# The last projection of a hybrid mLSTM / differential-attention block with its operands exchanged, and the high parts of the weight tiles on ScalarE

## The reference, cut to what matters

```python
xn   = rmsnorm(x, pre_g)
proj = xn @ w_in                      # 1024 x 10256, split into the parts used below
h_a  = sigmoid(m_o) * rmsnorm(mlstm_forward + mlstm_backward) * silu(m_z)      # 4 heads
h_b  = rmsnorm(diff_attention(aq, ak, av)) * (1 - lam_init) * silu(a_z)        # 8 heads
g_a, g_b = split(sigmoid(g_merge + b_merge))
y    = g_a * (h_a @ w_branch_m) + g_b * (h_b @ w_branch_a)
out  = y @ w_out                      # 1024 x 1024: the last projection
return x + rmsnorm(out, post_g)       # norm over the 1024 channels of each token
```

## Time and profile before

| | us |
|---|---|
| median of three runs | 1740.48 |
| profiled execution, whole | 1740.36 |
| its span in the trace | 1738.6 |
| TensorE matmul busy | 1655.1 (95%) |
| VectorE busy | 1037.4 (60%) |
| ScalarE busy | 755.8 (43%) |
| GpSimd busy | 771.0 (44%) |

### The profile page before, as it was taken

The page is one execution under the profiler, slowest core; times in us unless marked ns, Lnnn a source line. Parts: engine busy times, 40 slices in busy tenths (PEclk is TensorE's granted clock), DMA queues, the critical chain, the costliest instruction groups (busy, mean ns, idle before and its releaser), DMA issues.

```text
span 1738.6 us, 24563 instructions
## 1 busy us (share of the span) xinstructions
PE 1655.1 (95%) x8235; PEld 1355.8 (78%) x8235; DVE 1037.4 (60%) x1692; ACT 755.8 (43%) x1462; POOL 771.0 (44%) x926
## 2 busy tenths in 40 slices
PE   4999999999999998999999999999999999999995
PEld 3788887887878877878787878787877788888784
DVE  6703676776676767787878787878776101235213
ACT  5213444444444434555555555555554113344322
POOL 3543244244253355444444454545432444567630
PEclk9999999999999999999999999999999999999998
DMA  5041112012022022121212121212121737523322
GB/s 169 13 134 30 31 49 73 24 51 70 24 60 61 25 86 61 37 61 40 57 41 55 42 54 45 52 45 51 48 61 49 254 128 259 169 74 95 121 72 97
DMA packets 137300, 129.08 MB, mean 74 GB/s; under 512 B 5089, under 2 KB 120354, under 8 KB 136226
## 3 DMA queue, kind: packets, MB, share of 16 engines
q1 hardware_dynamic: 130594, 111.66, 22.1%
q10 hardware_dynamic: 6656, 16.78, 2.5%
HBM read 90.67 MB, written 29.36 MB: 69 GB/s over the span
## 4 chain that ended last, share of the span: by engine, by line
PE 60%; DVE 19%; ACT 10%; issue 10%; DMA 1%; DVEq 1%; ACTq 0%; SPq 0%
PE ps L621 45%; PE ps L629 7%; DVE negmax L1351 2%; PE ps L803 2%; PE ps L811 2%; ACT probs L1794 2%; ACT aT_split L1799 2%; DVE aT_split L1356 1%; DMA v_f<-in_x 1%; DVE h_sum L1304 1%; DVE raw_b L1038 1%; DVE mix L1343 1%; DVE q_stack L1286 1%; DVE sigmoid_work L1038 1%; DVE h_sum L1234 1%
## 5 line engine op out<-in xcount | busy, mean ns | idle before, releaser
L621 PE MATMUL ps<-xn_split,w_split 128*128 128x512 f32 x4224 | 1032.9, 401 | 2.4 <-ACT v_f L1501 1.9
L621 PEld LDWEIGHTS ps<-xn_split,w_split 128*128 128x128 f32 x4224 | 789.5, 189 | 187.1 <-POOL w_split L560 2.3
L554 POOL TENSOR_TENSOR w_split<-w_raw,ones 128x256 fp32r<-128x256 f32 x416 | 318.8, 796 | 855.9 <-PE ps L621 812.8
L560 POOL TENSOR_TENSOR w_split<-w_raw,w_split 128x256 fp32r<-128x256 f32 x416 | 329.3, 822 | 8.2
L1794 ACT ACTIVATE probs<-ps,negmax 128x1024 f32<-128x1024 f32 x128 | 143.0, 1117 | 139.0 <-DVE negmax L1351 139.0
L621 PE MATMUL ps<-h_split,w_split 128*128 128x512 f32 x768 | 181.2, 396 | 0.1
L621 PEld LDWEIGHTS ps<-h_split,w_split 128*128 128x128 f32 x768 | 143.4, 188 | 35.1 <-issue 0.5
L1351 DVE TENSOR_REDUCE negmax<-ps 128x1 f32<-128x1024 f32 x128 | 150.2, 1214 | 4.5 <-PE ps L803 4.5
L1356 DVE TENSOR_TENSOR aT_split<-ps,aT_split 128x512 fp32r<-128x512 f32 x128 | 88.5, 691 | 90.5 <-ACT aT_split L1799 89.6
L803 PE MATMUL ps<-k_stack,q_stack 128*128 128x512 f32 x512 | 135.7, 407 | 7.0 <-DMA k_stack<-k_stack 7.0
L803 PEld LDWEIGHTS ps<-k_stack,q_stack 128*128 128x128 f32 x512 | 92.4, 191 | 25.7 <-DMA k_stack<-k_stack 5.4
(11 more groups left out here) (236 smaller groups left out, 1843.8 us busy)
## 6 DMA issues: line engine op xcount, KB each, us to landing
w_raw<-in_w_in SPq DMA_DIRECT2D x80, 512.0 KB, 3.9
k_stack<-k_stack SPq DMA_DIRECT2D x16, 512.0 KB, 4.2
spill_a<-o_split SPq DMA_DIRECT2D x32, 256.0 KB, 2.8
h_split<-spill_m SPq DMA_DIRECT2D x8, 1024.0 KB, 7.1
qk_f<-spill_g SPq DMA_DIRECT2D x16, 512.0 KB, 3.4
xn_split<-spill_a SPq DMA_DIRECT2D x8, 1024.0 KB, 6.9
spill_g<-qk_f ACTq DMA_DIRECT2D x12, 512.0 KB, 2.6
spill_m<-hT_split ACTq DMA_DIRECT2D x8, 512.0 KB, 2.9
```

The costliest lines, as they stand in the source:

```text
L554: hi = pool.tensor_tensor(wsp[b][:, 0, ks_], raw[b][:, ks_], ones[:, 0:1].unsqueeze(2).to_broadcast([P, SPLIT_K, P]), ALU.mult)
L560: lo = pool.tensor_tensor(wsp[b][:, 1, ks_], raw[b][:, ks_], wsp[b][:, 0, ks_].bitcast(F32), ALU.subtract)
L621: mm = pe.matmul(ps[:, half, :], wsp[b][:, wl, k, :], moving[:, xl, k, cols], start=(k == 0 and n == 0), stop=(k == KT - 1 and n == 2))
```

## The change

It has two parts.

**The last projection.** y is now the stationary operand, 128 tokens at a time, and w_out moves in quarters of 256 channels. Each of 32 units (quarter n, token tile t) has 24 matmuls of 256 columns and leaves tokens on partitions, so the copy to SBUF and the transposes back are gone. A quarter is made of two 128-channel tiles; GpSimd makes both their parts, into new buffers `wo[n % 2]` that lie where `ya` was. For quarter 0 it waits for four of eight y tiles, for quarter 1 for all eight, and for quarters 2 and 3 until TensorE is done with the quarter before the last. Eight PSUM banks are used in turn. Per unit VectorE multiplies by the gain and ScalarE squares and sums; in the last quarter each token tile gets its sum, its statistics, its scaling and its store two tiles behind the matmuls. The first six units begin with seven of eight y tiles.

**The high parts.** For tiles 2 to 95 the high part is one ScalarE copy of 128x1024 (`split_high`), issued right behind the read of the second half of tile g-2; GpSimd makes only the low part, and waits for that copy. SP's load of a tile waits for the low part of tile g-2, as before.

The core of the diff; AHEAD is 6, and the last loops shown are VectorE's and ScalarE's:

```diff
+            wo = [sb(f"wo_split{i}", [P, 2, KT, QUARTER], F32R, at=f_scope) for i in range(2)]
...
                 g, b = tile_no(base, per_head, h, j)
-                pool.wait_ge(raw_loaded[b], 16 * ((per_head // 2) * h + ((base + j) // 2 + 1)))
-                if not (isinstance(g, int) and g < 2):
+                if isinstance(g, int) and g < 2:
+                    pool.wait_ge(raw_loaded[b], 16)
+                    for k in range(0, KT, SPLIT_K):
+                        ks_ = slice(k, k + SPLIT_K)
+                        hi = pool.tensor_tensor(wsp[b][:, 0, ks_], raw[b][:, ks_],
+                                                ones[:, 0:1].unsqueeze(2).to_broadcast([P, SPLIT_K, P]), ALU.mult)
+                    hi.then_inc(w_first, 1)
+                    pool.wait_ge(w_first, g + 1)
+                else:
                     pool.wait_ge(proj_done, 2 * g - 2)
-                for k in range(0, KT, SPLIT_K):
-                    ks_ = slice(k, k + SPLIT_K)
-                    hi = pool.tensor_tensor(wsp[b][:, 0, ks_], raw[b][:, ks_],
-                                            ones[:, 0:1].unsqueeze(2).to_broadcast([P, SPLIT_K, P]), ALU.mult)
-                hi.then_inc(w_split, 1)
-                pool.wait_ge(w_split, 2 * g + 1)
+                    pool.wait_ge(w_high, g - 1)
                 for k in range(0, KT, SPLIT_K):
                     ks_ = slice(k, k + SPLIT_K)
                     lo = pool.tensor_tensor(wsp[b][:, 1, ks_], raw[b][:, ks_], wsp[b][:, 0, ks_].bitcast(F32),
                                             ALU.subtract)
...
+            def split_out(n, j):
+                g, b = G_O + 2 * n + j, j
+                cols = slice(j * P, (j + 1) * P)
+                pool.wait_ge(raw_loaded[b], 16 * (g // 2 + 1))
+                if n < 2:
+                    pool.wait_ge(y_lo, KT // 2 * (n + 1))
+                else:
+                    pool.wait_ge(o_done, ST * (n - 1))
+                for k in range(0, KT, SPLIT_K):
+                    ks_ = slice(k, k + SPLIT_K)
+                    hi = pool.tensor_tensor(wo[n % 2][:, 0, ks_, cols], raw[b][:, ks_],
+                                            ones[:, 0:1].unsqueeze(2).to_broadcast([P, SPLIT_K, P]), ALU.mult)
+                hi.then_inc(w_first, 1)
...
+                for k in range(0, KT, SPLIT_K):
+                    ks_ = slice(k, k + SPLIT_K)
+                    lo = pool.tensor_tensor(wo[n % 2][:, 1, ks_, cols], raw[b][:, ks_],
+                                            wo[n % 2][:, 0, ks_, cols].bitcast(F32), ALU.subtract)
+                lo.then_inc(w_low, 1)
...
+            def out_unit(n, t, begin=0, end=KT):
+                at = slice(t * P, (t + 1) * P)
+                for k in range(begin, end):
+                    for i, (yl, wl) in enumerate(PASSES):
+                        mm = pe.matmul(ps[:, bank_of(t), 0:QUARTER], ys[:, yl, k, at], wo[n % 2][:, wl, k, :],
+                                       start=(k == 0 and i == 0), stop=(k == KT - 1 and i == 2))
+                if end == KT:
+                    mm.then_inc(o_done, 1)
+
+            pe.wait_ge(w_low, G_O + 2)
             pe.wait_ge(y_lo, KT - 1)
+            for t in range(AHEAD):
+                out_unit(0, t, end=KT - 1)
+            pe.wait_ge(y_lo, KT)
+            for t in range(AHEAD):
+                out_unit(0, t, begin=KT - 1)
+            pe.wait_ge(proj_read, 2 * G_O)
+            for t in range(AHEAD, ST):
+                out_unit(0, t)
+            for n in range(1, QUARTERS):
+                pe.wait_ge(w_low, G_O + 2 * n + 2)
+                for t in range(ST):
+                    pe.wait_ge(o_squares, ST * (n - 1) + t + 1)
+                    out_unit(n, t)
...
+            for t in range(ST):
+                rows(QUARTERS - 1, t)
+                if t > 0:
+                    row_total(t - 1)
+                if t > 1:
+                    dve.wait_ge(o_rows, ST * (QUARTERS - 1) + t - 1)
+                    finish(t - 2)
+            row_total(ST - 1)
+            for t in (ST - 2, ST - 1):
+                dve.wait_ge(o_rows, ST * (QUARTERS - 1) + t + 1)
+                finish(t)
...
+            def split_high(base, per_head, h, j):
+                _, b = tile_no(base, per_head, h, j)
+                act.wait_ge(raw_loaded[b], 16 * ((per_head // 2) * h + ((base + j) // 2 + 1)))
+                act.activation(wsp[b][:, 0], raw[b][:], ACT.Copy).then_inc(w_high, 1)
...
                 else:
                     act.activation(dst, ps[:, half, :], ACT.Identity, bias=bias).then_inc(proj_read, 1)
+                if half == 1 and not (base == G_FB and is_last(h)):
+                    split_high(base, per_head, h, j + 2)
...
+            def row_squares(n, t):
+                act.wait_ge(o_rows, ST * n + t + 1)
...
+                act.activation(junk_row[:, slot * QUARTER:(slot + 1) * QUARTER], ps[:, bank_of(t), 0:QUARTER], ACT.Square,
+                               accum_out=tile_sums[:, t, n:n + 1]).then_inc(o_squares, 1)
```

More of the change, by code:

```diff
@@ L82, in prep_act_at, with is_last @@
     return PREP_ACT.index(name) + 1
+def is_last(c):
+    return isinstance(c, int) and c == KT // 2 - 1
 def is_zero(h):
@@ L894, in _, with bank_of @@
                         proj_half(base, 2, c, j, 1, moving=h)
[L897 to L907, removed]
+            def bank_of(t):
+                return (t + 2) % 8
@@ L1478, in _, with bank_of, rows @@
-            with dve.Fori(0, KT // 2) as c2:
-                for par in range(2):
-                    rows(2 * c2 + par, par)
-            dve.wait_ge(res_loaded, 16 * ST)
-            dve.wait_ge(o_stat, 2)
-            dve.wait_ge(o_rows, 2 * KT)
-            for t in range(ST):
+            def bank_of(t):
+                return (t + 2) % 8
+            def rows(n, t):
+                cols = slice(n * QUARTER, (n + 1) * QUARTER)
+                dve.wait_ge(o_done, ST * n + t + 1)
+                dve.tensor_tensor(orow[:, t, cols], ps[:, bank_of(t), 0:QUARTER], post_bc[:, cols],
+                                  ALU.mult).then_inc(o_rows, 1)
@@ L1921, in _ @@
+            def merge(n, base):
+                with act.Fori(0, KT // 2 - 1) as c:
+                    merge_pair(n, base, c)
+                merge_pair(n, base, KT // 2 - 1)
             merge(0, G_FA)
             merge(1, G_FB)
-            def out_tile(c, par):
-                if not (isinstance(c, int) and c < 2):
-                    act.wait_ge(o_tr, 2 * c - 2)
-                for half in range(2):
-                    act.wait_ge(proj_done, 2 * (G_O + c) + half + 1)
-                    act.activation(outT[par][:, half * HALF:(half + 1) * HALF], ps[:, half, :],
-                                   ACT.Copy).then_inc(proj_read, 1)
@@ new lines, in row_rstd @@
+            def row_rstd(t):
+                act.wait_ge(o_sums, t + 1)
+                act.activation(tail_stat[:, t:t + 1], row_sums[:, t:t + 1], ACT.Ln, bias=eps[:],
+                               scale=1.0 / D).then_inc(o_stat, 1)
+                act.wait_ge(o_stat, 2 * t + 1)
+                act.activation(tail_stat[:, t:t + 1], tail_stat[:, t:t + 1], ACT.Exp, scale=-0.5).then_inc(o_stat, 1)
+            for n in range(QUARTERS):
+                for t in range(ST):
+                    row_squares(n, t)
+                    if n == QUARTERS - 1 and t > 0:
+                        row_rstd(t - 1)
```

129 lines of the change are left out of this document (54 added, 75 removed).

## The result

The changed kernel took 1722.13 us, median of four runs (1721.58 to 1722.89), against 1740.03 (1738.78 to 1741.96) for the one before on the same chip: ratio 0.9896, 95% interval 0.9879 to 0.9914. Faster by 1.0%; 1724.0 had been forecast. The profiled execution has a span of 1720.7 us, 17.9 less than before.

What follows compares the result with a forecast made beforehand. TensorE's work, its waits and what follows its last matmul were taken to bound the kernel; -16.2 + 19.3 - 7.7 - 9.2 - 1.9 - 0.7 = -16.4 us gave 1724.0 us from 1740.48, range 1711 to 1740.

Steps and rivals of the forecast that it cites:

- term 3: Attention head starts: less GpSimd work relieves VectorE, cutting 1.1 us of TensorE's 2.13 wait in seven heads; -7.7 us.
- terms 4 and 6: mLSTM head ends (-9.2 us) and first attention head's keys (-0.7): VectorE, relieved of GpSimd contention, shortens TensorE's waits.
- Term 1: Last projection: 4.8 us from TensorE's rate, the rest from its start and a shorter end; -16.2 us.
- rival d: Last projection: quarter 0 or 1 late because GpSimd still makes both w_out parts; +4 to +6, 1729 us; chance 0.10.
- Rival e: Last projection: the doubled loads are not hidden behind the moving passes; +35, 1759 us; chance 0.03.
- Term 2: Attention: ScalarE copies behind halves 1, 3 and 5 delay TensorE, 2.35 us per head; +19.3 us over eight heads.
- The fourth copy: Attention: the last of a head's four copies, behind half 7, falls where ScalarE idles.
- Term 6: First attention head: TensorE's wait for keys that VectorE makes under GpSimd's splits shrinks; -0.7 us.
- rival c: Attention and mLSTM: ScalarE becomes what TensorE waits for at each block; 1756 us; chance 0.06.
- Term 5: Preparation: TensorE's wait of 2.34 us for GpSimd at 74.85 shrinks; -1.9 us.
- rival b: VectorE's relief doesn't come, as GpSimd's low parts move into the same VectorE instructions; 1737 us; chance 0.13.
- rival a: Attention: the copies find ScalarE's idle time, term 2 at its lower end; 1713 us; chance 0.14.

Runs made afterwards that it cites:

- Experiment 7: Changed kernel with each matmul of the last projection as two of 128 columns: 1802.49 us, ratio 1.0355 to the kernel before.
- experiment 5: As experiment 2, but the copy behind half 7 stays on ScalarE: 1704.83 us, ratio 0.9795 to the kernel before.
- experiment 2: Changed kernel with the high parts of the 34 tiles made during attention back on GpSimd: 1707.74 us, ratio 0.9812 to the kernel before.
- Experiment 8: From experiment 4, the copy behind half 7 goes behind the first `high_round` of the next head: 1695.01 us, ratio 0.9741 to the kernel before.
- experiment 6: Changed kernel with the high parts of tiles 2 to 95 left out altogether: 1706.96 us, ratio 0.9803 to the kernel before.
- experiment 4: Changed kernel, attention's copies behind halves 1, 3 and 5 moved behind the next block's first `high_round`: 1703.7 us, ratio 0.979 to the kernel before.
- experiment 3: Changed kernel, attention's copies behind halves 1, 3 and 5 issued one block later, behind the exponentials: 1723.51 us, ratio 0.99 to the kernel before.

## Why the prediction was right

The total was 1.9 us too high. The mechanisms of the large terms came as written, one step of term 3 failed, and three terms had the wrong size. Measured less forecast, the terms are off by -0.7, -2.0, +4.5, -3.5 (terms 4 and 6) and +0.6 us, in sum -1.1 (the stretches of the table give -1.5): that the total came so near is in part luck.

- **Term 1, -16.2; measured -16.9.** The loads took 92.3 us for the forecast 91.8. From the last of them to the end of the span it is 7.6 us, forecast 8.8 (1722.4 less 1713.6). Quarters 0 and 1 were in time (rival d fell), but quarter 1 by 1.1 us only: it was ready at 1642.66, where 1641.3 had been worked out, though the stage began 1.0 us earlier. Its first load was issued at 1625.33 and GpSimd began on it at 1632.26, 6.9 us later; the 3.9 of the earlier trace rows had been taken. Rival e fell too: 0.120 us a pair, as the PV rows said. Experiment 7 shows how near it was: at half the columns a pair still takes 0.112, so if that is the load, at 256 columns the move covers it with little to spare. The Trainium skill's figures (TensorE: Matmul & The Clock Gate, Back-to-back issue gap; 81 ns at 128 columns, 131 at 512) fit neither end here: 112 was measured at 128 columns, 120 at 256, 230 at 512.
- **Term 2, +19.3; measured +17.3** in the waits for `aT_split` (29.9 to 47.2). The step that said all of a copy's 0.95 lands on TensorE is right: in the head of the earlier trace rows the waits behind the copies of halves 1, 3 and 5 went from 0.76, 0.39 and 0.35 to 1.16, 1.29 and 1.29, by 0.40, 0.90 and 0.94 where 0.45, 0.95 and 0.95 had been forecast. The fourth copy was free, as said (experiment 5).
- **Term 3, -7.7; measured -3.2 to -4.3** (waits named "issue", 14.3 to 11.1 us; seven times 0.56 is 3.9; attention in experiment 5 less that in experiment 2, 4.3). This step failed: "The low part will run from about 1002.8, so it is over by then". Measured from L1423 (1005.65 before, 999.22 after) the low part began at 1003.0 on the old time, as said, but it took 3.34 us there and ended at 1006.4, 0.7 after L1423 had begun. So L1423 kept its 1.00, and of the 1.1 us only its successor's share came (L1409, 0.95 to 0.41). The two in front of it even grew, from 0.73 and 0.72 to 0.85 and 0.84, since the low part now lies over them; the two on `q_stack` before those (L1286, now L1328) shrank, from 2.77 to 2.47 together. In sum that is 0.6, the 0.56 measured. Experiment 8 moved the low part away and got 1.28 a head: the contention was there to be removed, and what removed it was the place of the low part.
- **Terms 4 and 6, -9.9; measured -13.4.** All of both waits went, where I had kept 0.9 of the second: I had counted the scalings' gain only up to the first wait. But the two waits measure one lateness of VectorE, 1.30 + 2.17 = 3.5 us in total. Its chain from the start of the scalings to the start of `hT_f` (L1246, at 394.03 before; L1288, at 383.55 after) went from 25.85 to 22.69 us: 2.06 less in the scalings, 0.7 in six convolution instructions and 0.8 in small ones around them, and 0.4 more in L1180 (1.28 before, 1.65 after), over which the low part now lies. Term 6, the wait for keys in front of the first scores of attention, is 4.99 to 4.44, 0.55 for the forecast 0.7. The copies are hidden, so rival c fell (experiment 6). The scalings have one SBUF data input. The Trainium skill (SBUF — State Buffer, Who interferes with whom, Practical consequences) says that such an instruction doesn't contend with GpSimd, but excepts the modes that use both ports, and names `tensor_scalar`; 0.53 each beside GpSimd and 0.27 alone agree with the exception.
- **Term 5, -1.9; measured -1.3,** though the first TensorE work came 0.6 us later in this execution (38.47 for 37.90). The wait of 2.34 is 1.34.
- **Rivals a and b.** Neither happened: no idle slot in ScalarE took the three copies where they were put, and the relief came, though GpSimd's work went from 771 to 483 us, less than the near half that was held against rival b. But both point at something real. The slots of rival a exist 2 us further on (experiment 4), and in experiment 3 the low parts did move into VectorE's instructions, as rival b had it.

The overhead around the span is as it was: the profiled execution took 1722.57 us whole, 1.9 more than its span of 1720.7, before 1.8.

## What to carry to other kernels

Work moved to another engine has two places to look at: where it stands in that engine's order, and when the work that waits for it will run, and beside what. Here the same 32 copies cost 14 us net behind a read that TensorE waits for, and no less one block on, because of what they released; in gaps that suited both, the kernel was 18 us faster with three of four moved and 27 with all. When VectorE and GpSimd share a stage, a delay of GpSimd's work can be worth more than the removal of a part of it: at the head's start taking the high part away gave 2.9 us (experiment 5 against 2), and moving the low part by 12 us gave 8.7 (experiment 8 against 4).

## What had not been expected of the hardware

- A VectorE instruction with one SBUF data input was slowed by about the same factor as those with two: 128x256 scalings 0.53 us beside GpSimd and 0.27 alone, 128x256 `tensor_tensor` 0.85 to 1.01 beside it and 0.42 alone.
- The collision stretches both sides and by different amounts: GpSimd's low part takes 2.8 us alone and 3.3 to 5.5 beside VectorE, and a 128x1024 mix 1.28 alone, 1.76 to 2.19 beside it.
- For this type and these blocks a pair of load and move takes 0.112 us at 128 columns and 0.120 at 256. So half the columns save 0.008 us a pair; nothing between the two was measured.
